# Two pads in on-chip memory that shift the buffers which TensorE reads

## The chip, the cores and the metric

The kernel runs on one core of one Trainium2 chip. The metric is the device time of one execution in microseconds; the three runs of the kernel before took 944.46, 943.92 and 945.84 us, median 944.46.

A core has TensorE (matrix products, with a separate load of the stationary operand ahead of each), VectorE, ScalarE, GpSimd and SyncE, which here issues the transfers. They share an on-chip memory of 128 partitions; a tensor takes the same range of bytes in every partition. In this text "+32" means: the tensor's first byte lies 32 bytes behind a multiple of 128.

## What is computed

Two transformer blocks in a row on 256 tokens of width 1024, in float32. The first block is a two-layer network, the second one layer with a gated linear attention. Cut to its outline:

```python
def first_block(x, ...):
    h = x
    for layer in range(2):
        if layer < 1:
            h = h + short_conv_mixer(rms_norm(h, ...), a_w_in, a_conv, a_w_out)   # 1024 -> 3072 -> 1024
        else:
            h = h + mla_attention(rms_norm(h, ...), b_w_dq, ..., k_nope, v, k_rope, cos, sin)  # 8 heads
        h = h + conv_ffn(rms_norm(h, ffn_norm[layer]), ...)                        # 1024 -> 5632, conv, 2816 -> 1024
        if layer == 0:
            shared = shared_latent_kv(h, ...)
    return rms_norm(h, final_norm)

def second_block(x, c, ctx, ...):
    # modulation from c @ ada_w; context of 256 tokens
    a_lat, a_ctx = modulate(rmsnorm(h_lat, ...), ...), modulate(rmsnorm(h_ctx, ...), ...)
    _, o_lat = gla_mixer(a_ctx, a_lat, ...)            # 4 heads, both directions, chunks of 64
    h_lat = h_lat + mod_l[2] * o_lat
    h_lat = h_lat + mod_l[5] * sqrelu_mlp(modulate(rmsnorm(h_lat, ...), ...), mlp_w1, mlp_w2)   # 1024 -> 4096 -> 1024
    return rmsnorm(h_lat, final_g)
```

## The kernel before

Activations are kept feature-major: 128 features per chunk on the partitions, 256 tokens beside each other, so a chunk is 1024 bytes per partition and chunk k of a buffer begins k x 1024 bytes behind its start.

The weights come as a stream of "units" of 128 x 1024 float32, each of eight 128 x 128 blocks, into a ring of four slots (`raw`). ScalarE rounds a unit to the product's format (`whi`, line 1007), VectorE takes the rest (`wlo`, line 1528). Activations are split the same way into a hi and a lo buffer. A block product is then three matmuls: whi with the hi activation, whi with the lo, wlo with the hi (lines 498, 499 and 502, helper `units`), each with the weight block stationary and the 256 tokens moving. A unit is therefore 24 matmuls. Every matmul loads its own stationary operand. `looped` runs the same helper in a hardware loop; the two-layer network's up projections are 44 units each, the down projections 24 units with 22 blocks per output tile, so 528 matmuls.

Variants of it:

- Lines 477 to 481, 596 to 602, 651 to 653, 713 to 715 and 904 to 906 are the same three matmuls in another order over chunks or heads.
- Where a value matrix is wanted token-major (helper `moving`, lines 530 to 532), an activation chunk is stationary and 512 weight columns move.
- In the MLP (helper `units` with `both`, lines 501 and 502) the hi and lo halves of the activations, which lie in one buffer, move in one matmul of 2 x 256 columns, and a narrow matmul with wlo follows.
- The first units of the MLP (lines 958 to 960) read `uhi`, whose chunks are 258 columns (1032 bytes) long.
- Scores, attention values, statistics and the decays of the gated attention are plain float32 matmuls.

The order on every engine is written out by hand; engines wait for each other by semaphores. Transfers of weights are issued by SyncE as slots of `raw` come free.

On-chip tensors are placed one behind another in the order of the `sb(...)` calls, each size rounded up to 32 bytes; an `ExitStack` that is closed gives its range back, so tensors of different stages overlap. `sb` is called with a number of 4-byte columns. The program has no other say in an address. The places that matter, in bytes within a partition:

| tensors | begins before | behind a multiple of 128 | after | behind a multiple of 128 |
|---|---|---|---|---|
| raw, whi, wlo, h | 1152, 17536, 33920, 50304 | +0 | the same | +0 |
| ct (tables) | 60224 | +64 | the same | +64 |
| wa2r, t1, rstd, ssum, sq | 72032 ... 81248 | +96 | the same | +96 |
| state | 88096 | +32 | the same | +32 |
| x (hi and lo) | 96288 | +32 | 96384 | +0 |
| y, o, q, k, kn, vv, c, E, ki, kz, gv, m, ... | 112672 and on | +32 | 96 further | +0 |
| cv, sil, prod, side | 161856 and on | +64 | 96 further | +32 |
| rt_tab, c32, rstd_c | 195200 and on | +0 | 96 further | +96 |
| z (hi, lo) | 210048, 218240 | +0 | 210176, 218368 | +0 |
| uhi, ulo | 186400, 194656 | +32, +96 | 96 further | +0, +64 |

Of the kernel before, what the change touches and what calls it, by code (L numbers as in the profile page):

```python
# [17 lines left out]
F32 = mybir.dt.float32  # L18
# [159 lines left out]
def program(nc, stream, xT, ctxT, vec, cst, rot, wa2, crow, out):  # L178
    ctx = ExitStack()

    def sb(name, cols, dt=F32, stack=ctx, rows=P):
        return stack.enter_context(nc.sbuf_tensor(name, [rows, cols], dt))

    with ctx:
# [19 lines left out]
        ee = sb("ee", 4 * GH)  # L204
        state = sb("state", 2 * GH * T)

        stage = ExitStack()
        x2 = sb("x2", 2 * DC * T, F32R, stage)
        xhi, xlo = x2[:, 0:DC * T], x2[:, DC * T:2 * DC * T]
        stage.close()  # L210
        stage = ExitStack()
# [3 lines left out]
        stage = ExitStack()  # L215
# [7 lines left out]
        stage = ExitStack()  # L223
# [4 lines left out]
        stage = ExitStack()  # L228
# [3 lines left out]
        stage = ExitStack()  # L232
# [26 lines left out]
        stage = ExitStack()  # L259
        sb("stacks_held", EARLY, F32, stage)  # L260
        rt_tab = sb("rt_tab", NROT, F32, stage)
        c32 = sb("c32", DC * T, F32, stage)
        rstd_c = sb("rstd_c", T, F32, stage)
        zhi = sb("zhi", DC * T, F32R, stage)
        zlo = sb("zlo", DC * T, F32R, stage)
        stage.close()
        stage = ExitStack()
# [22 lines left out]
        stage = ExitStack()  # L290
# [2092 lines left out]
```

How the kernel before makes its waits and increments, by code:

```python
    def take(self, sem, by=1):  # L140
        self.n[sem.name] = self.n.get(sem.name, 0) + by
        self.eng.wait_ge(sem, self.value(sem))
# [6 lines left out]
    def again(self, sem, back=0):  # L150
        if self.n.get(sem.name, 0) - back > 0:
            self.eng.wait_ge(sem, self.value(sem, -back))
# [207 lines left out]
        @block.sync  # L361
# [1 line left out]
            def load_group(first, done):  # L363
                for j in range(RING):
                    sp.wait_ge(slots_done, done + (j + 1))
                    sp.dma_start(raw[:, j * D:(j + 1) * D], stream[first + j]).then_inc(raw_ready[j], 16)
# [15 lines left out]
            def load_next(p):  # L382
                sp.wait_ge(slots_done, p - RING + 1)
                sp.dma_start(raw[:, p % RING * D:(p % RING + 1) * D], stream[p]).then_inc(raw_ready[p % RING], 16)
# [11 lines left out]
            def load_down(first, last):  # L396
                for p in range(first, last):
                    load_next(p)
                    kind, u = ORDER[p]
                    if kind == "w" and u in SIDE_BEHIND:
                        s = SIDE_BEHIND[u]
                        if s >= SIDE:
                            sp.wait_ge(side_done, s - SIDE + 1)
                        sp.dma_start(side[:, s % SIDE * D:(s % SIDE + 1) * D], stream[POSITIONS + s])\
                            .then_inc(side_ready[s % SIDE], 16)
# [13 lines left out]
                sp.wait_ge(ev("out_chunk"), n + 1)  # L420
                sp.dma_start(out[:, first * T:last * T], h[:, first * T:last * T]).then_inc(ev("stored"), 16)
            sp.wait_ge(ev("stored"), 16 * len(OUT_PARTS))
```

## Time and profile before

| | |
|---|---|
| median of the runs | 944.46 us |
| span of the profiled execution, first to last instruction | 944.4 us |
| its mean granted TensorE clock | 0.997 |
| TensorE matmuls | 933.6 us busy, 6952 instructions |
| TensorE weight loads | 889.8 us busy, 6952 instructions |
| VectorE | 798.0 us busy |
| ScalarE | 564.0 us busy |

The profile gives no duration of the execution beyond the span; the median is 0.1 us above it. Busy time counts overlapping instructions once. A matmul's duration in the profile reaches over the starts of the next ones, so the cost of a matmul in a stream is the distance between starts, to be had from the timeline or from the number of matmuls that a window holds.

### The profile page before, as it was taken

What the parts mean: (1) busy time and instruction counts of PE and PEld (TensorE: products, weight loads), DVE (VectorE), ACT (ScalarE), POOL (GpSimd) and SP (SyncE); (2) the same over time, 40 slices, a digit from 0 to 9 for tenths busy, and PEclk for the clock granted to TensorE, in tenths of its full rate; (3) what the DMA queues carried; (4) which work ended last, traced back from release to release, by engine and by line L of the source; (5) the groups of instructions that cost most, each with busy time, mean ns of one, the idle gap of its engine ahead of it and who ended that gap; (6) DMA issues with size and microseconds to landing.
All of it is one profiled execution on the core that took longest, in us unless ns stands there. A gap on an engine that the chain in (4) does not pass through costs nothing.

```text
span 944.4 us, 19749 instructions
## 1 busy us (share of the span) xinstructions
PE 933.6 (99%) x6952; PEld 889.8 (94%) x6952; DVE 798.0 (85%) x1317; ACT 564.0 (60%) x934; POOL 1.8 (0%) x8
## 2 busy tenths in 40 slices
PE   9999999999999999999999999999999999999997
PEld 8999999999999999999999999988899988888886
DVE  6999899999989888899999987955868889886553
ACT  6645656666455665766666556977533668674342
POOL 0000000000000000000000000000000000000000
PEclk9999999999999999999999999999999999999998
DMA  8776575557776554565557765563674348776661
GB/s 296 245 268 229 184 273 193 195 181 277 250 269 208 174 180 157 179 199 179 183 192 269 250 241 180 175 225 134 222 252 173 112 158 265 234 236 223 180 199 44
DMA packets 53877, 195.49 MB, mean 207 GB/s; under 512 B 6110, under 2 KB 6366, under 8 KB 53696
## 3 DMA queue, kind: packets, MB, share of 16 engines
q1 hardware_dynamic: 53680, 193.72, 61.5%
q10 hardware_dynamic: 144, 1.05, 0.3%
q8 instruction: 35, 0.57, 0.2%
q14 instruction: 18, 0.15, 0.0%
HBM read 193.69 MB, written 1.05 MB: 206 GB/s over the span
## 4 chain that ended last, share of the span: by engine, by line
PE 94%; DVE 4%; ACT 1%; issue 1%; DVEq 0%; ACTq 0%
PE ps L502 25%; PE ps L498 20%; PE ps L499 19%; PE ps L501 10%; PE ps L530 2%; PE ps L532 2%; PE ps L531 2%; DVE wlo L1528 1%; PE ps L609 1%; PE ps L792 1%; PE ps L808 1%; PE ps L651 1%; PE ps L652 1%; PE ps L653 1%; PE ps L674 1%
## 5 line engine op out<-in xcount | busy, mean ns | idle before, releaser
L1528 DVE TENSOR_TENSOR wlo<-raw,whi 128x1024 fp32r<-128x1024 f32 x303 | 367.0, 1220 | 72.9 <-ACT whi L1007 71.8
L1007 ACT ACTIVATE whi<-raw 128x1024 fp32r<-128x1024 f32 x303 | 317.0, 1052 | 90.8 <-PE ps L502 58.9
L502 PE MATMUL ps<-x,wlo 128*128 128x256 f32 x1248 | 349.5, 280 | 0.0
L498 PE MATMUL ps<-x,whi 128*128 128x256 f32 x1024 | 289.1, 282 | 0.0
L499 PE MATMUL ps<-x,whi 128*128 128x256 f32 x1024 | 286.9, 280 | 0.0
L502 PEld LDWEIGHTS ps<-x,wlo 128*128 128x128 f32 x1248 | 234.9, 188 | 0.0
L498 PEld LDWEIGHTS ps<-x,whi 128*128 128x128 f32 x1024 | 192.8, 188 | 0.8 <-issue 0.2
L499 PEld LDWEIGHTS ps<-x,whi 128*128 128x128 f32 x1024 | 192.8, 188 | 0.6 <-issue 0.5
L502 PE MATMUL ps<-yhi,wlo 128*128 128x256 f32 x400 | 112.1, 280 | 0.0
L498 PE MATMUL ps<-yhi,whi 128*128 128x256 f32 x400 | 112.1, 280 | 0.0
L499 PE MATMUL ps<-ylo,whi 128*128 128x256 f32 x400 | 112.1, 280 | 0.0
L1053 ACT ACTIVATE cv<-U,vt 128x256 f32<-128x256 f32 x88 | 44.9, 511 | 85.4 <-DVE U L1672 85.4
L501 PE MATMUL ps<-x,whi 128*128 128x512 f32 x224 | 78.1, 393 | 1.0 <-DVE mr L2212 0.6
L501 PE MATMUL ps<-m,whi 128*128 128x512 f32 x224 | 77.7, 392 | 0.0
L498 PEld LDWEIGHTS ps<-yhi,whi 128*128 128x128 f32 x400 | 75.3, 188 | 0.0
L499 PEld LDWEIGHTS ps<-ylo,whi 128*128 128x128 f32 x400 | 75.3, 188 | 0.0
L502 PEld LDWEIGHTS ps<-yhi,wlo 128*128 128x128 f32 x400 | 75.3, 188 | 0.0
L502 PE MATMUL ps<-m,wlo 128*128 128x256 f32 x256 | 71.6, 280 | 0.0
L501 PEld LDWEIGHTS ps<-x,whi 128*128 128x128 f32 x224 | 42.0, 188 | 11.0 <-DVE wlo L1528 1.0
L501 PEld LDWEIGHTS ps<-m,whi 128*128 128x128 f32 x224 | 42.1, 188 | 9.3
L502 PEld LDWEIGHTS ps<-m,wlo 128*128 128x128 f32 x256 | 48.0, 188 | 0.0
L1570 DVE SCALAR_TENSOR_TENSOR cv<-U,vt,cv 128x256 f32<-128x256 f32 x96 | 45.9, 479 | 0.6 <-ACT cv L1153 0.6
(333 smaller groups left out, 1536.6 us busy)
## 6 DMA issues: line engine op xcount, KB each, us to landing
raw<-stream SPq DMA_DIRECT2D x343, 512.0 KB, 4.0
side<-stream SPq DMA_DIRECT2D x16, 512.0 KB, 4.7
h<-xT SPq DMA_DIRECT2D x2, 512.0 KB, 6.1
c<-ctxT ACTq DMA_DIRECT2D x1, 1024.0 KB, 6.2
out<-h SPq DMA_DIRECT2D x4, 256.0 KB, 2.4
ct<-cst SPq DMA_DIRECT2D x1, 898.5 KB
rt_tab<-rot SPq DMA_DIRECT2D x1, 704.0 KB
state<-crow SPq DMA_DIRECT2D x1, 512.0 KB, 6.5
```

What stands on the lines that cost most here:

```text
L498: pe.matmul(dst, whi[:, w], at(hi, k), start=(k == 0), stop=False)
L499: pe.matmul(dst, whi[:, w], at(lo, k), start=False, stop=False)
L501: pe.matmul(ps[t % lag][:, :], whi[:, w], halves_of(both, k), start=(k == 0), stop=False)
L502: last = pe.matmul(dst, wlo[:, w], at(hi, k), start=False, stop=(k == K - 1))
L530: pe.matmul(dst, hi[:, tok], whi[:, w], start=first, stop=False)
L531: pe.matmul(dst, lo[:, tok], whi[:, w], start=False, stop=False)
L532: last = pe.matmul(dst, hi[:, tok], wlo[:, w], start=False, stop=final)
L609: pe.matmul(ps[7][:, 0:T], U[:, 0:P], U[:, 0:T], start=True, stop=True)
L1007: c.sig(act.activation(whi[:, s * D:(s + 1) * D], raw[:, r * D:(r + 1) * D], ACT.Copy), hi_ready)
L1053: c.sig(act.activation(at(cv, j), U[:, j * (T + 2) + 2:(j + 1) * (T + 2)], ACT.Copy, scale=vt_col(i * 12 + (base + 3 * j + 2))), tap_ready)
L1528: c.sig(dve.tensor_tensor(wlo[:, w], raw[:, r], whi[:, w], ALU.subtract), slots_done)
L1570: c.sig(dve.scalar_tensor_tensor(out=at(cv, j), in0=U[:, o + 1:o + T + 1], scalar=w1, in1=at(cv, j), op0=ALU.mult, op1=ALU.add), seq_dve)
```

## The change

Two tensors are declared that nothing reads or writes: 24 columns (96 bytes) ahead of the stage buffers, and 8 columns (32 bytes) ahead of z.

```diff
@@ -204,6 +204,7 @@
         ee = sb("ee", 4 * GH)
         state = sb("state", 2 * GH * T)
 
+        sb("line_pad", 24)
         stage = ExitStack()
         x2 = sb("x2", 2 * DC * T, F32R, stage)
         xhi, xlo = x2[:, 0:DC * T], x2[:, DC * T:2 * DC * T]
@@ -261,6 +262,7 @@
         rt_tab = sb("rt_tab", NROT, F32, stage)
         c32 = sb("c32", DC * T, F32, stage)
         rstd_c = sb("rstd_c", T, F32, stage)
+        sb("z_pad", 8, F32, stage)
         zhi = sb("zhi", DC * T, F32R, stage)
         zlo = sb("zlo", DC * T, F32R, stage)
         stage.close()
```

The instructions of every engine and their order are the same before and after, and only addresses differ; in the profile after, a line behind the first pad has a number higher by one, behind the second by two. The table above lists the addresses. Not every operand of a product ends at a multiple of 64: the tables, the gate's weights and inputs, the sums of squares and the state keep their places, the rotary table goes from +0 to +96, and the chunks of uhi begin 1032 bytes apart.

## Rows read from the trace of the kernel before

**Rows 1.** The page: busy time, TensorE's granted clock in 40 slices, the chain by engine.

```profile
PE 933.6 (99%) x6952; PEld 889.8 (94%) x6952; DVE 798.0 (85%) x1317; ACT 564.0 (60%) x934; POOL 1.8 (0%) x8
...
PEclk9999999999999999999999999999999999999998
...
PE 94%; DVE 4%; ACT 1%; issue 1%; DVEq 0%; ACTq 0%
```

**Rows 2.** Waits of TensorE: total us, times, longest.

```profile
PE ps L609 <- DVE U L1792: 2.0, 1, 2.0
PE ps L567 <- ACT sq L1500: 0.7, 1, 0.7
```

**Rows 3.** TensorE's groups by form: count, busy us, mean ns.

```profile
L502 PE MATMUL ps<-x,wlo 128*128 128x256 f32 x1248 | 349.5, 280 | 0.0
...
L530 PE MATMUL ps<-whi,zhi 128*128 128x512 f32 x48 | 19.0, 395 | 0.0
...
L530 PE MATMUL ps<-whi,x 128*128 128x512 f32 x32 | 12.8, 400 | 0.0
```

**Rows 4.** Windows, TensorE alone: length, busy (count), clock, DMA share, GB/s.

```profile
104.50:224.50 120.00, 120.00 (x1025) 1.00 0.63 213
...
370.00:381.00 11.00, 11.00 (x94) 1.00 0.49 161
391.00:511.00 120.00, 120.00 (x1013) 1.00 0.58 193
...
658.00:676.00 18.00, 18.00 (x81) 1.00 0.51 171
740.30:754.50 14.20, 14.20 (x121) 1.00 0.54 179
800.00:900.00 100.00, 100.00 (x579) 1.00 0.69 219
924.60:935.50 10.90, 10.90 (x95) 1.00 0.00 0
```

**Rows 5.** Timeline, start and duration: z moving; a pair in the MLP.

```profile
749.90 0.28 PE L502 MATMUL ps<-zhi,wlo 128*128 128x256 f32 x1
...
750.98 0.28 PE L502 MATMUL ps<-zhi,wlo 128*128 128x256 f32 x1
...
849.78 0.39 PE L501 MATMUL ps<-m,whi 128*128 128x512 f32 x1
850.01 0.28 PE L502 MATMUL ps<-m,wlo 128*128 128x256 f32 x1
```

**Rows 6.** Weight loads by tile: ns min/median/max, first and last start.

```profile
L498 PEld LDWEIGHTS ps<-zhi,whi x48: 188/192/192, 576.1 to 754.2; 128*128 128x128 f32 x48
...
L904 PEld LDWEIGHTS ps<-zhi,whi x24: 186/192/193, 730.5 to 739.8; 128*128 128x128 f32 x24
...
L498 PEld LDWEIGHTS ps<-x,whi x1024: 187/188/193, 15.1 to 716.3; 128*128 128x128 f32 x171
```

**Rows 7.** Timeline, starts of wide matmuls, x and then z stationary.

```profile
623.60 0.40 PE L530 MATMUL ps<-whi,x 128*128 128x512 f32 x1
...
624.77 0.40 PE L532 MATMUL ps<-wlo,x 128*128 128x512 f32 x1
...
670.16 0.39 PE L530 MATMUL ps<-whi,zhi 128*128 128x512 f32 x1
...
671.29 0.39 PE L532 MATMUL ps<-wlo,zhi 128*128 128x512 f32 x1
```

**Rows 8.** VectorE's groups by form: count, busy us, mean ns.

```profile
L1615 DVE SCALAR_TENSOR_TENSOR raw<-raw,cr 128x1024 f32<-128x1024 f32 x32 | 38.8, 1219 | 0.0
...
L1633 DVE SCALAR_TENSOR_TENSOR side<-side,cr 128x1024 f32<-128x1024 f32 x16 | 19.2, 1220 | 0.0
...
L2019 DVE SCALAR_TENSOR_TENSOR x<-a,mod,x 128x256 fp32r<-128x256 f32 x16 | 7.3, 480 | 0.8 <-ACT x L1285 0.8
...
L1748 DVE SCALAR_TENSOR_TENSOR c<-c,gmod,rstd_c 128x256 f32<-128x256 f32 x8 | 3.8, 480 | 0.0
```

## The prediction

> **What bounds the kernel now.** I read the page first: TensorE is busy for 933.6 of 944.4 us at a granted clock of 2.4 GHz almost throughout, and the chain of waits runs over it for 94% [rows 1]. The waits of TensorE confirm it: the longest is 2.0 us, at the very start, and the later ones are at most 0.7 us [rows 2]. So it does not matter here how early data is ready. What matters is the distance from one matmul's start to the next. The groups by form give the counts: nearly all matmuls are "narrow" (256 moving columns, a weight block stationary) in the triples of lines 498, 499 and 502, and they differ only in the activation buffer that they read (the largest group, line 502 with x, has 1248) [rows 3]. Their mean of 280 ns is no cost, since they overlap. The distance comes from the windows: a window of length L that holds nothing but such matmuls counts about (L + 0.28)/c of them, the 0.28 us being one that began before it. That gives, from [rows 4]:
>
> - 104.5 to 224.5 us, x moving, first up projection: 120.28/1025 = 117.3 ns
> - 391 to 511, x moving, second up projection: 120.28/1013 = 118.7
> - 370 to 381, o moving: 11.28/94 = 120.0
> - 740.3 to 754.5, z moving: 14.48/121 = 119.7, or 120 by its starts: 749.90 to 750.98 holds nine distances of 120 ns [rows 5]
>
> **The experiment that before already holds.** The weights whi and wlo begin at a multiple of 128 bytes. x, y, o, c, k and m begin 32 bytes behind one. z alone, of the activations, begins at a multiple of 128. So z shows today what the others will be after. It shows two things.
>
> First, as moving operand z is not faster. It runs at 120 ns, against 117.3 and 118.7 for most of the others. The weight loads say the same: those ahead of z's narrow matmuls have a median of 192 ns in each of its stages; those of x have 188 [rows 6]. That a buffer at +32 reached 120 too, in one stretch, says that 120 is one of several steady cycles. z's narrow matmuls have it in all their stages (576 to 754 us), whatever ran before.
>
> Second, as stationary operand z is faster. Where the weights move (512 columns, lines 530 to 532), x gives starts at 623.60 and 624.77 with five distances between them, 234 ns each. z gives 670.16 and 671.29, 226 ns each [rows 7]; the means by form differ the same way, 400 to 395 ns [rows 3].
>
> **The change part by part.** No instruction is added, dropped or moved on any engine, and no wait. The first pad shifts every tensor behind `state` by 96 bytes; the second is 32 bytes and brings z to a multiple of 128 again. So the whole price is in durations.
>
> *Narrow matmuls*, which go from +32 to +0. Counts are from the units, 24 matmuls each. I take 120 ns for all of them, as z has.
>
> - Until 295 us: 24 + 8 + 44 + 22 + 3 = 101 full units' worth, 2424 matmuls, 117.35 to 120: 2424 x 2.65 ns = +6.4 us
> - 295 to 388 us (the latents, queries and o): 480 matmuls, partly at 120 already, so between 0 and +1.3; I take +0.6
> - 390 to 576 us: 44 + 22 units, 1584 matmuls at 118.7: x 1.3 ns = +2.1
> - 590 to 722 us: x in 17 units, 408 matmuls, at the rate of the stage before: +0.5
> - the last four units (924.6 to 935.5, 11.18/95 = 117.7 ns): 96 x 2.3 = +0.2
>
> Together +9.8 us.
>
> *Wide matmuls with an activation stationary*: x 96 and k 24 go from 234 to about 227 (18.39/81 in 658 to 676 [rows 4]): 120 x -7 ns = -0.8 us.
>
> *The MLP*, 448 pairs of one wide (both halves moving) and one narrow matmul, lines 501 and 502. The pair takes 2 x 100.34/579 = 346.6 ns [rows 4], of which the wide has about 230 [rows 5] and so the narrow 117. At +0 I expect the narrow at 120 and the wide at 227, which gives 347 again: 0. If only the narrow one changes: 448 x 2.6 = +1.2. If only the wide one does: 448 x -3 = -1.3.
>
> *Other products*: fp32 ones (scores, values, statistics) keep their cost. The raw units' uhi has chunks of 1032 bytes, so its chunks stay off the line whatever the buffer's start; ct, t1, ssum, sq and state stay at +32 to +96 as well, since they lie ahead of the pad. I put 0 on them, and +-0.2 at most for ulo, which moves from +96 to +64.
>
> *VectorE and ScalarE*: cv, sil, prod and side go from +64 to +32 and c32 from +0 to +96. The rows show no price for a start. Three-operand products of 128x256 take 480 ns on c (+0), 480 on x (+32); products of 1024 take 1220 on side (+64) and 1219 on raw (+0) [rows 8]. ScalarE is busy for 60% only [rows 1]. So 0, and TensorE's slower pace would cover some ns anyway; without that cover, one ns on each of VectorE's 1317 instructions would be 1.3 us.
>
> Sum: 9.8 - 0.8 = +9.0 us. Nothing covers it, as TensorE is the bound. The profiled execution spans 944.4 us, 0.1 under the median of 944.46, so I add to the latter: **953.5 us**.
>
> **A rule against it.** Rows 7 show that a start at +32 and one at +0 give different distances for a stationary operand. The Trainium skill (SBUF — State Buffer, Specifications) puts the line of on-chip memory at 16 bytes and charges for each crossing to a new line. All starts here, before and after, are multiples of 32, so by that rule the pads change nothing, and the time stays 944.5. The trace disagrees for the stationary operand (234 against 226 ns); for the moving one it leaves the rule a chance, below.
>
> **The rivals.**
>
> *No difference* (0.2). The cycle is set by how a stretch was entered and not by the address. For it: the same buffer x at the same address runs at 117.3 in the first block and at 118.7 in the second, and o, also at +32, at 120.0 [rows 4]. Against it: z was entered several times, after fp32 products and after wide ones, and has 120 in all of them [rows 6]. Then only the stationary gain is left, and the MLP at 0: 943.7 us. The cadences of the first block stay at 117.3. The time that the rule above gives lies within 0.2% as well.
>
> *Faster* (0.25 in all). It is one mechanism: a moving operand that begins at a multiple of 128 bytes takes less time, as a stationary one does, and z's 120 is a coincidence of its stage. Its place is every narrow matmul, and it decides if the distance at +0 is under 117.3. The mild form: all stages settle at 117.3. Then 390 to 576 us gives -2.1, o and the latents -0.6, the x units -0.5, z's 216 x -2.6 = -0.6, the stationary ones -0.8, the MLP -1.3: -5.9 us, 938.6 us. The strong form: each narrow matmul saves the 7 ns that the stationary operand shows, on 4992 + 216 of them and the MLP's 448: about -40 us, 905 us. Against both stands that z shows the opposite. I give the mild one 0.2 and the strong one 0.05.
>
> *The MLP is hit too*, inside the forecast: 954.7; or the wide one gains: 952.2.
>
> **How the numbers follow.** Forecast 0.55, no difference 0.2, faster 0.25. About 0.2%, 1.9 us, is what a measurement can tell here. The forecast is wholly above it, "no difference" wholly within, so slower 0.55, same 0.2, faster 0.25. The forecast's own range is 949 (only the first block changes) to 955.5 (the MLP's narrow ones, the upper bound of 295 to 388 us, and noise). With "no difference" and the upper edge of the mild gain the range is 941 to 955.5; what is left out is the rest of "faster", about 0.2.
>
> **What would show it.** In the profile after, the window 104.5 to 224.5 should count about 1002 matmuls instead of 1025, and the starts there should be evenly 0.12 us apart. The weight loads of x should have a median of 192 ns. Lines 530 to 532 with x should stand 0.226 us apart, and a pair in the MLP at 0.347. The forecast is wrong if the count in that window is 1025 or more; if it is, the time is 944 or below. It is also wrong if z, now at +256 of 512 instead of +128, leaves 120.

## The result and the profile after

| | before | after |
|---|---|---|
| median of 6 runs | 945.83 us (943.92 to 947.93) | 957.92 us (954.83 to 958.49) |
| ratio | | 1.0123, 95% interval 1.0105 to 1.0141 |
| span of the profiled execution | 944.4 us | 956.4 us |

The change makes the kernel slower by 1.2%. The six runs of after lie at two levels, 954.8 to 954.9 and 957.6 to 958.5; the profiled execution took 958.23 us, so it is one of the upper level. Its time is 1.8 us longer than its span.

The page of after, against [rows 1]:

```profile
PE 945.8 (99%) x6952; PEld 899.8 (94%) x6952; DVE 799.3 (84%) x1317; ACT 563.8 (59%) x934; POOL 1.8 (0%) x8
...
PE 94%; DVE 4%; ACT 1%; issue 1%; DVEq 0%; ACTq 0%
```

The counts are the same and TensorE is busy for 12.2 us more; the other engines' busy time changed by at most 1.3 us. So the matmuls stand further apart. The windows over the same stretches of work, moved on by what the kernel has lost until there, answer to [rows 4]:

```profile
106.50:226.50 120.00, 120.00 (x1002) 1.00 0.62 209
376.50:387.50 11.00, 11.00 (x94) 1.00 0.47 164
400.00:520.00 120.00, 120.00 (x1002) 1.00 0.57 190
668.00:686.00 18.00, 18.00 (x79) 1.00 0.52 171
812.00:912.00 100.00, 100.00 (x568) 1.00 0.65 216
```

The first and the third hold 1002 narrow matmuls where before had 1025 and 1013: 120.28/1002 = 120.0 ns in both blocks, and the starts are evenly 0.12 us apart. The second, o moving, was at 120 already. The weight loads agree: x's median is now 192 ns, as z's was in [rows 6], and z's has fallen to 188:

```profile
L500 PEld LDWEIGHTS ps<-x,whi x1024: 188/192/192, 15.2 to 725.5; 128*128 128x128 f32 x171
```

```profile
L500 PEld LDWEIGHTS ps<-zhi,whi x48: 187/188/192, 584.7 to 763.2; 128*128 128x128 f32 x48
...
L906 PEld LDWEIGHTS ps<-zhi,whi x24: 186/188/192, 739.6 to 749.0; 128*128 128x128 f32 x24
```

z was to stay as it was, since it begins at a multiple of 128 before and after. It did not. Where [rows 5] had 120 ns, the 119 distances between these two starts are 118.7 ns each:

```profile
749.44 0.28 PE L500 MATMUL ps<-zhi,whi 128*128 128x256 f32 x1
...
763.56 0.28 PE L504 MATMUL ps<-zhi,wlo 128*128 128x256 f32 x1
```

x and z have changed roles as stationary operands too (line 532 of after, which is line 530 of before: 397 ns with x and 400 with z, where [rows 3] had 400 and 395); z's wide stage holds 79 matmuls in 18 us where it held 81.

The last window is the other surprise: the pair of the MLP takes 2 x 100.34/568 = 353.3 ns, where before had 346.6. Its timeline, against [rows 5]:

```profile
859.79 0.40 PE L503 MATMUL ps<-m,whi 128*128 128x512 f32 x1
860.03 0.28 PE L504 MATMUL ps<-m,wlo 128*128 128x256 f32 x1
860.15 0.40 PE L503 MATMUL ps<-m,whi 128*128 128x512 f32 x1
860.39 0.28 PE L504 MATMUL ps<-m,wlo 128*128 128x256 f32 x1
860.50 0.40 PE L503 MATMUL ps<-m,whi 128*128 128x512 f32 x1
860.73 0.28 PE L504 MATMUL ps<-m,wlo 128*128 128x256 f32 x1
860.85 0.40 PE L503 MATMUL ps<-m,whi 128*128 128x512 f32 x1
```

Three pairs take 1.06 us, and it is the wide one that grew. Over the starts of the whole down half of the MLP its mean distance to the narrow one behind it is 236.0 ns, where before had 229.2; the narrow one's is 117.3, where before had 117.5.

Where the 12 us between the two spans went, from the starts of the same instruction in the two traces (in us; stretches by the time of before):

| stretch | before | after | difference |
|---|---|---|---|
| 7.8 to 296.7, first block's narrow | 288.92 | 295.35 | +6.4 |
| 296.7 to 391, attention | 94.42 | 94.58 | +0.2 |
| 391 to 576, second block's narrow | 184.64 | 186.72 | +2.1 |
| 576 to 768, gated attention | 192.5 | 192.9 | +0.4 |
| 768 to 923, the MLP's pairs | 154.89 | 157.67 | +2.8 |
| 923 to 936, its last narrow ones | 12.53 | 12.82 | +0.3 |

### The profile page after: what moved, and what is told of

Its sections match the earlier page's. It is cut to its first block, busy times and chain, and to the rows that moved or that the text cites. A ratio compares the mean times of both kernels' runs of the same rounds, so it can differ in the third digit from the quotient of the medians.

```text
span 956.4 us, 19749 instructions
## 1 busy us (share of the span) xinstructions
PE 945.8 (99%) x6952; PEld 899.8 (94%) x6952; DVE 799.3 (84%) x1317; ACT 563.8 (59%) x934; POOL 1.8 (0%) x8
## 4 chain that ended last, share of the span: by engine, by line
PE 94%; DVE 4%; ACT 1%; issue 1%; DVEq 0%; ACTq 0%
PE ps L504 25%; PE ps L500 20%; PE ps L501 20%; PE ps L503 10%; PE ps L532 2%; PE ps L534 2%; PE ps L533 2%; DVE wlo L1530 1%; PE ps L611 1%; PE ps L794 1%; PE ps L810 1%; PE ps L653 1%; PE ps L654 1%; PE ps L655 1%; PE ps L676 1%
## 5 line engine op out<-in xcount | busy, mean ns | idle before, releaser
L504 PEld LDWEIGHTS ps<-x,wlo 128*128 128x128 f32 x1248 | 238.8, 191 | 0.0
L501 PEld LDWEIGHTS ps<-x,whi 128*128 128x128 f32 x1024 | 196.5, 192 | 0.6 <-issue 0.5
L500 PEld LDWEIGHTS ps<-x,whi 128*128 128x128 f32 x1024 | 196.5, 192 | 0.6 <-issue 0.5
L503 PEld LDWEIGHTS ps<-x,whi 128*128 128x128 f32 x224 | 42.1, 188 | 12.0 <-DVE wlo L1530 0.8
```

The lines of the kernel that those rows point to most:

```text
L500: pe.matmul(dst, whi[:, w], at(hi, k), start=(k == 0), stop=False)
L501: pe.matmul(dst, whi[:, w], at(lo, k), start=False, stop=False)
L503: pe.matmul(ps[t % lag][:, :], whi[:, w], halves_of(both, k), start=(k == 0), stop=False)
L504: last = pe.matmul(dst, wlo[:, w], at(hi, k), start=False, stop=(k == K - 1))
```

## The experiments

In all of them a tensor's "distance" is where it begins behind the place of the weights (whi; wlo has the same), modulo 256 bytes. It isn't to be mixed up with the distance of starts in time, which is given in ns and is called the pace below; a pace that a stretch of matmuls keeps is a steady cycle. Before: x, y, o, c, k, m at 160, z at 0. After: x, y, o, c, k, m at 0, z at 128.

**A map of distances.** All work is left out but the three patterns of products, on two large buffers, the activation's start moved by 32 bytes from one section to the next; each section is 96 narrow, 36 wide or 48 pair matmuls behind a short float32 product. VectorE and ScalarE do nothing while they run, and next to nothing is transferred (0 to 3 GB/s, where the long stages of the kernel have about 200).

```python
for kind, ws, xs in plan():
    w0, xb = 8 * ws, x0 + 8 * xs        # columns of 4 bytes
    pe.matmul(ps[6][:, 0:64], ones[:, :], ones[:, 0:64], start=True, stop=True)
    ...
    pe.matmul(dst, W[:, w], X[:, hi], start=(k == 0), stop=False)
    pe.matmul(dst, W[:, w], X[:, lo], start=False, stop=False)
    pe.matmul(dst, W[:, wl], X[:, hi], start=False, stop=(k == 7))
```

> Leaves out the whole computation: it only runs the three patterns of products (narrow triples, wide with the activation stationary, pairs of the MLP) with the activation buffer begun at 16 places 32 bytes apart (0 to 480 bytes behind the weights' place, modulo 512), and the narrow one also with the weights moved on by 128, 256 and 384 bytes. Theory 'distance' (what counts is where the moving operand begins against where the stationary one does, modulo 256 or 512): narrow 120 ns at distance 0 and 118.7 or less at the others; with the weights moved by 128 the 120 moves with them, to activations at +128. Theory 'place' (the activation's own place modulo 512 counts): the 120 stays at the same activation place whatever the weights do. Theory 'multiple of 128' (my prediction's): 120 at 0, 128, 256 and 384 alike. Wide: 227 ns at distance 0, 233 at 128 by both of the first theories, 227 at both by the third. Pair: 353 ns at distance 0 and 346.6 at 416 (where before had it).

The rows are the products between the sections, in order of time; the distances are 0, 32, 64, ... 224 bytes, each from one row to the next:

```profile
28.68 0.33 PE L75 MATMUL ps<-ones 128*128 128x64 f32 x2
40.41 0.33 PE L75 MATMUL ps<-ones 128*128 128x64 f32 x2
51.85 0.33 PE L75 MATMUL ps<-ones 128*128 128x64 f32 x2
63.38 0.33 PE L75 MATMUL ps<-ones 128*128 128x64 f32 x2
75.12 0.33 PE L75 MATMUL ps<-ones 128*128 128x64 f32 x2
86.86 0.33 PE L75 MATMUL ps<-ones 128*128 128x64 f32 x2
98.48 0.33 PE L75 MATMUL ps<-ones 128*128 128x64 f32 x2
109.59 0.33 PE L75 MATMUL ps<-ones 128*128 128x64 f32 x2
121.17 0.33 PE L75 MATMUL ps<-ones 128*128 128x64 f32 x2
```

The 96 matmuls take 11.73 us at distance 0, 11.44 at 32 and 11.11 at 192. The mean pace in each section, without its first matmuls, in ns (a pair counts as one):

| distance | 0 | 32 | 64 | 96 | 128 | 160 | 192 | 224 |
|---|---|---|---|---|---|---|---|---|
| narrow, first sweep | 120.0 | 116.7 | 117.8 | 120.0 | 120.0 | 118.7 | 113.3 | 118.3 |
| narrow, other order | 120.0 | 116.7 | 117.8 | 120.0 | 118.7 | 118.7 | 117.8 | 118.3 |
| wide, activation stationary | 226.7 | 233.3 | 233.3 | 234.4 | 233.3 | 233.3 | 228.9 | 233.3 |
| pair | 353.3 | 346.7 | 353.3 | 350.1 | 351.1 | 346.8 | 353.3 | 353.5 |

The values for 256 to 480 bytes repeat these in the first sweep for narrow and wide. (In the other order 288 gave 117.8 where 32 gave 116.7, and the pair gave 346.7 at 256 where it gave 353.3 at 0.) With the weights moved on by 128, 256 or 384 bytes, the six sections at distance 0 all have 120.0, and the six at 128 have 118.7 or 120.0; the activations at their first place have 120.0 with the weights at theirs and 118.7 once the weights are 128 on. So the place alone is out, and so is a multiple of 128: distance 0 has 120.0 in every section, whatever the two places, and 128, as much a multiple of 128 as 0 is, has 118.7 in half of its sections. It isn't a sharp test, since 128 has 120.0 in the other half; moving only the weights in the kernel, below, is one. The expectation "118.7 or less at the others" failed: 96 has 120.0 in both sweeps. Two values for the same two addresses (at 128, 192 and 288) are what no theory of addresses alone allows. As the other engines stand still here, a clash with their reads and writes is not what makes these differences.

**The second pad left out.**

```diff
-        sb("z_pad", 8, F32, stage)
```

> One part alone: the first pad stays, the second is left out, so z begins at +32 (224 of 512) and all else is as after. Theories 'distance' and 'place': z's narrow matmuls at 117.3 to 118.7 ns and its wide ones at 231 to 233, about as after (118.7 and 232.5), so the time is within 0.5 us of after. 'Multiple of 128': z after and before should have been alike, which the profile after already denies; under it nothing is forecast.

957.0 us, ratio 1.012 (1.0086 to 1.0154) over before, so the first pad alone carries the loss. One thing came out otherwise than expected: z, now at distance 96, has 120.0 ns as moving operand (100 distances between the starts at 749.40 and 761.41), not 117.3 to 118.7, which is what the map has for 96. Its profile fell on a run of the lower level (955.52 us, span 953.7), and the MLP, whose buffers lie exactly where after has them, is as fast as before:

```profile
809.50:909.50 100.00, 100.00 (x578) 1.00 0.70 221
```

That is 347 ns for a pair, at the address that has 353.3 in after. In the down half the wide one is at 231.8 and the narrow one at 114.8 ns. So the same instructions at the same addresses have two paces in two executions, though of kernels that differ in z's place.

**The second pad alone**, with z put where after has it:

```diff
+        sb("z_pad", 32, F32, stage)
         zhi = sb("zhi", DC * T, F32R, stage)
```

> The other part alone: before, with 128 bytes ahead of z, so that z begins at a multiple of 128 (256 of 512), as after, and all else is as before. If the second pad costs what the traces show in z's wide stages (48 x 3 matmuls at +5.5 ns, +0.8 us) less what z's narrow ones give back (216 x -1.3 ns, -0.3 us), the time is +0.5 us over before; x at 117.3 and 118.7 as before, the MLP's pair at 346.6. Theory 'multiple of 128': no difference at all.

946.17 us, ratio 1.000 (0.9981 to 1.0019): no difference that can be measured. By the starts, z's wide stages lost 0.7 us and its narrow one gained 0.2, as expected. The profile, of a run of 947.12 us, also held what was not: until 103 us x and y, at their unchanged places, ran at 118.7 ns where the trace of before has 117.3, and from there at before's pace; the stretch from 7.8 to 103 us took 1.5 us longer. And o, also unmoved, ran at 117.3 ns where before had 120.0.

**Everything moved by 128 bytes**, the weights too:

```diff
+        sb("first_pad", 32)
         raw = sb("raw", RING * D)
```

> After, with 128 more bytes ahead of the very first buffer: all buffers, the weights' too, move on by 128, distances stay. Theory 'distance': as after, narrow x at 120.0 ns in all stages, the MLP's pair at 353.3, time within 0.5 us of after. Theory 'place': x is now at 256 of 512, where z had 118.7 ns after, so narrow x at 118.7 (4992 x -1.3 ns = -6.5 us) and a changed pair.

956.28 us, ratio 1.0103 (1.0069 to 1.0137). The four runs lie at after's two levels, 954.94 and 955.01, 957.54 and 957.95, so the median says little here; level by level they are within 0.5 us of after. The trace, of a run of 957.54 us, has after's windows, and its pairs in the MLP are at 353.3 ns:

```profile
106.50:226.50 120.00, 120.00 (x1002) 1.00 0.61 210
400.00:520.00 120.00, 120.00 (x1002) 1.00 0.57 191
```

**Distances and entries.** The map again, with the float32 product ahead of a section varied in width:

```python
ENTRIES = (64, 33, 97, 128, 17, 80)
for kind, d, e in plan():
    pe.matmul(ps[6][:, 0:e], ones[:, :], ones[:, 0:e], start=True, stop=True)
```

> Leaves out the whole computation, as the first map did. Each of the 8 distances 0 to 224 bytes modulo 256 (where the activations begin behind the weights' place) is entered six times for narrow triples and four times for pairs, each time behind a float32 product of another width (64, 33, 97, 128, 17, 80 columns); between 160 and 224 bytes there are also steps of 8 bytes. Theory 'distance and entry' (a distance allows one or several steady cycles, and the entry picks one): distance 0 always at 120 for narrow, 192 at 113.3 in some entries and 117.8 in others, 128 at 120 or 118.7; the pair at distance 0 at 353.3 in some and 346.7 in others, at 32 and 160 always at 346.7. Theory 'distance alone': the same value for all entries of a distance, and the second sweep of the first map then has no explanation.

| distance | settled values over the entries, ns |
|---|---|
| narrow 0 | 120.0 six times |
| narrow 32, 64, 96 | 116.7; 117.8; 120.0, each six times |
| narrow 128 | 120.0 twice, 118.7 four times (rounded) |
| narrow 160 | 118.7 seven times (rounded), 117.3 once, 120.0 once |
| narrow 192 | 117.8 six times (rounded), 113.3 three times |
| narrow 168, 184, 200 | 120.0, three times each |
| pair 0 | 353.3 once, 346.7 three times (rounded) |
| pair 32, 160 | 346.7 four times each |
| pair 192 | 353.3 four times |

The rows around distance 192 with entry widths 64 and 33, and around the pair at 0 with the same two:

```profile
63.44 0.33 PE L78 MATMUL ps<-ones 128*128 128x64 f32 x2
69.31 0.33 PE L78 MATMUL ps<-ones 128*128 128x64 f32 x2
...
110.66 0.30 PE L78 MATMUL ps<-ones 128*128 128x33 f32 x2
116.33 0.30 PE L78 MATMUL ps<-ones 128*128 128x33 f32 x2
...
471.61 0.33 PE L78 MATMUL ps<-ones 128*128 128x64 f32 x2
477.48 0.33 PE L78 MATMUL ps<-ones 128*128 128x64 f32 x2
...
518.27 0.30 PE L78 MATMUL ps<-ones 128*128 128x33 f32 x2
524.04 0.30 PE L78 MATMUL ps<-ones 128*128 128x33 f32 x2
```

The same 48 matmuls at the same addresses take 5.87 or 5.67 us, the same 32 of the pairs 5.87 or 5.77. A distance has one steady pace or several. What picks one isn't shown: it isn't the width of the product ahead alone, since 97 columns led to 117.8 ns at 192 in one section and to 113.3 in another, and in the kernel the pair's pace differs between executions with the same addresses. 160, where before has its buffers, has all three that the trace of before showed: 117.3, 118.7 and 120.0. For narrow matmuls this is the second half of the "no difference" rival, true for 160 and false for 0; the pair has two paces at 0.

**Buffers at 192**, the MLP's inner buffer at 32, as an edit of after:

```diff
-        sb("line_pad", 24)
+        sb("line_pad", 8)
-        sb("z_pad", 8, F32, stage)
+        sb("z_pad", 40, F32, stage)
+        sb("m_pad", 24, F32, stage)
         m2 = sb("m2", 2 * MC * T, F32R, stage)
```

> Pads chosen so that x, y, o, c and z begin 192 bytes behind the weights' place modulo 256 and the MLP's inner buffer and the raw units' at 32. Theory 'distance and entry': if the stages are entered into the 113.3 ns cycle, 4992 narrow matmuls gain 4.0 to 5.4 ns each, about -22 us, x's wide ones -0.5 us, the MLP's upper pairs (224, at 353.3) cost +1.5: about -21 us, 925 us. If all are entered into 117.8: about +1.0 in the first block, -1.4 in the second, +1.5 in the MLP, so +1 us. Theory 'distance alone' with the map's first value: 925 us. If the first pad's cost had nothing to do with the distance: 945 to 957.

944.25 us, ratio 0.9986 (0.9971 to 1.0001): the second case. The windows give 120.28/1020 = 117.9 and 120.28/1021 = 117.8 ns:

```profile
104.50:224.50 120.00, 120.00 (x1020) 1.00 0.64 211
391.00:511.00 120.00, 120.00 (x1021) 1.00 0.58 194
```

The 113.3 ns pace exists, and the long stages did not fall into it. Short ones did, x from 591 to 602 us for one, where the 54 distances between these starts are 113.3 ns each:

```profile
592.00 0.28 PE L481 MATMUL ps<-x,whi 128*128 128x256 f32 x1
...
598.12 0.28 PE L502 MATMUL ps<-x,whi 128*128 128x256 f32 x1
```

No way to steer into it was found. The MLP's upper pairs are at 353.3 and its lower ones at 346.7, as the map has it for 192 and 32.

**Buffers at 32**, as an edit of after:

```diff
-        sb("line_pad", 24)
+        sb("line_pad", 32)
-        sb("z_pad", 8, F32, stage)
+        sb("z_pad", 40, F32, stage)
```

> Pads chosen so that x, y, o, c, z, the MLP's inner buffer and the raw units' all begin 32 bytes behind the weights' place modulo 256. Theory 'distance and entry': narrow at 116.7 or 117.8 in every stage, the MLP's pair at 346.7, x's wide ones at 233. Against before at 117.3 and 118.7 that is -0.6 or +0.5 ns on the first block's 2424, -2.0 or -0.9 on the second's 1584: between -6 and -0.5 us, and +1 us for z's wide ones; so 939 to 946 us.

940.61 us, ratio 0.9958 (0.9937 to 0.998): faster than both kernels, with both blocks at 120.28/1031 = 116.7 ns and the pair at 346.6:

```profile
104.50:224.50 120.00, 120.00 (x1031) 1.00 0.65 217
391.00:511.00 120.00, 120.00 (x1031) 1.00 0.60 199
800.00:900.00 100.00, 100.00 (x579) 1.00 0.69 221
```

**Only the weights moved.** Before, with the activations left at their places modulo 256:

```diff
+        sb("first_pad", 40)
         raw = sb("raw", RING * D)
...
         state = sb("state", 2 * GH * T)
+        sb("line_pad", 24)
```

> Before, with 160 bytes ahead of the weights' ring and 96 behind `state`, so that the activations keep their places modulo 256 (x at +32 of 128, z at +0) and only the weights and what lies between move, by 160: x, y, o, k and m are then at distance 0 from the weights' place, though none of them begins at a multiple of 64. Theory 'distance': narrow at 120.0 ns in all stages, as after, x's wide ones at 227, and 955 to 958.5 us. Theory that a multiple of 128 or the activation's own place causes it: as before, 117.3 and 118.7 ns, 944 to 946 us.

957.03 us, ratio 1.0134 (1.0112 to 1.0157). In it x, y, o, c, k and m begin 32 bytes behind a multiple of 128, as in before, and it is as slow as after. Its trace (of a run at the lower level, 955.88 us) has after's windows for the narrow matmuls and before's pace in the MLP, 2 x 100.34/579 = 346.6 ns for a pair:

```profile
106.50:226.50 120.00, 120.00 (x1002) 1.00 0.62 209
400.00:520.00 120.00, 120.00 (x1002) 1.00 0.57 190
809.50:909.50 100.00, 100.00 (x579) 1.00 0.69 220
```

**The inner buffer at 32.** After, with one more pad:

```diff
+        sb("m_pad", 8, F32, stage)
         m2 = sb("m2", 2 * MC * T, F32R, stage)
```

> After, with 32 bytes more ahead of the MLP's inner buffer alone, which then begins 32 bytes behind the weights' place modulo 256. Theory 'distance and entry': the pairs of the MLP's down half (224) stay at 346.7 ns however they are entered, and only those of the up half can be at 353.3; the slow ones of the runs are then 1.5 us above the fast ones instead of 3, so 954.9 and 956.4 us, and 96 narrow ones gain 0.3 us. If the two levels of the runs after have another cause than the pairs: 954.9 and 958.3 as before this edit.

Four runs: 955.96, 956.02, 956.07 and 956.53 us, all within 0.5 us of the 956.4 forecast for slow upper pairs, none at 958. In the profile the first window is in the up half and the second in the down half:

```profile
783.00:843.00 60.00, 59.85 (x339) 1.00 0.78 243
862.00:922.00 60.00, 60.00 (x348) 1.00 0.63 203
```

**The changed kernel once more**, unedited:

> The changed kernel again, beside the two others on the same chip, for its levels: 954.9 and 958.3 us in the runs so far. In the profile the MLP's pairs are at 353.3 ns if its time is near 958.3 and at 346.7 if it is near 954.9; a time near 958.3 with pairs at 346.7 would make the theory of two cycles wrong for this difference.

957.70 to 957.75 us in four runs, ratio 1.0138 (1.012 to 1.0155), and both halves slow:

```profile
783.00:843.00 60.00, 59.85 (x339) 1.00 0.78 243
862.00:922.00 60.00, 60.00 (x341) 1.00 0.61 200
```

348 against 341 is the down half's pair at 346.7 ns against 353.3 by the starts: one pad of 32 bytes ahead of one buffer, 1.5 us. No run fell on the lower level here, so a profile of this very kernel at 954.9 us was not had; the one with the second pad left out and the one with only the weights moved stand for it. The link of the two levels to the pair rests on five traces with the activations at distance 0: the three at the upper level (957.54, 957.70 and 958.23 us) have 353.3, the two at the lower (955.52 and 955.88) have 346.7.

## Why the prediction was wrong

Its direction and its largest part were right, its size was not: 957.92 against 953.5, above the range's 955.5. Two steps make up nearly all of the 4.4 us, the MLP (2.8) and the base (1.4 by the medians). By its steps:

- **Narrow matmuls, +9.8 us.** Right in size: +6.4 in the first block and +2.1 in the second, to the digit. The attention gave +0.2 where I took +0.6. That 120 held was partly luck: z's 120 could be carried over to x only because x went to z's distance from the weights, which I did not look at.
- **The MLP, 0 with a bound of +1.2.** This step failed, by 2.8 us. I composed the pair from parts measured elsewhere (120 and 227) and bounded it by leaving one part unchanged. Neither bound allows a wide matmul that grows, and it went from 229.2 to 236.0 ns, with the narrow one at 117.3, in the traces of the upper level; in those of the lower it is 231.8 and 114.8. The pair is a pattern of its own with two paces at distance 0, 353.3 and 346.7 ns, and neither holds the 120 or the 227. At the lower level the MLP costs the 0 that I put on it, and the executions there (954.83 and 954.94) lie inside the range.
- **The base.** I took the span of 944.4 for the profiled execution's own time, 0.1 from the median. But 1.8 us of after's time lie outside its span, and 1.7 to 1.8 us in every later execution of before that has its time beside its span (946.15 us and 944.4, for one). So the profiled execution of before took about 946.2, and the sum of the trace belonged to that: 946.2 + 9.0 + 2.8 is 958.0, against 958.23. The median of before also moved from 944.46 to 945.83 with three more runs.
- **z stays, x's wide ones gain 0.8.** The gain came: k's wide matmuls at 317 us take 0.25 us less and x's at 623 us 0.4 less. But z did not stay: its wide ones lost 0.7 us, what its distance 0 had been worth, and its narrow ones gained about 0.3. The prediction named a z that leaves 120 as a sign that it is wrong.
- **VectorE, ScalarE: 0.** Right: 1217 and 1219 ns for the products on raw and side, 479 on c.

The reason behind the right term was wrong. I read z's 120 ns as the mark of a multiple of 128. z had two properties, a multiple of 128 and distance 0 from the weights, which began at a multiple of 128 as well. Moving the weights alone parts them, and the distance decides. The forecast of no difference that I drew from the rule of 16-byte lines in the Trainium skill (SBUF — State Buffer, Specifications) did not hold either: with every buffer's start at a multiple of 32, 32 bytes more ahead of one buffer take 1.5 us off the MLP's down half.

The rival "no difference" was right in its fact, that a buffer at one address runs at several paces, and wrong in its conclusion: for narrow matmuls that holds at 160, where before is, while 0 had 120.0 in every section and stage. "Faster" did not come, but pads that do it exist: 32 bytes more in the first and 128 more in the second, 0.4% under before.

What stays open: why a distance has the paces that it has, and what picks one. Before has more than one level too: its executions took 943.4 to 946.8 us, with a few at 948 to 950. A step of 2 us would fit 1584 matmuls at 117.3 or at 118.7 ns; that is argued, as both traces at hand with before's places for x (about 946.2 and 947.12 us) have 118.7 in the second block, and they differ in the first 103 us. That the long stages of a kernel keep to what the map's short sections show was tested at 0, 32, 160 and 192 only.

## What to carry to other kernels

When TensorE is the bound and every matmul loads its own weights, measure the distance of starts for each buffer pair before judging a layout, and sweep the distance between the two operands over 256 bytes in a kernel that runs nothing else, with more than one entry for each, and look in the kernel itself which of the paces its stages took; here that is what lies between a 1.2% loss and a 0.4% gain. Align to what was measured, not to a round number. Before a part seen in one stage is carried to another, ask what else it has in common with its neighbours, and do not compose a pattern's pace from the paces of its parts.

## What the runs showed of the hardware

- For 256 moving and 128 stationary float32 columns, with a weight load ahead of every matmul, the pace was 113.3 ns (at 192) to about 120.7 (at 216) by the distance of the operands' first bytes modulo 256, at a granted clock of 1.00 throughout.
- With the 512 weight columns moving, 226.7 ns at distance 0 and 228.9 to 234.4 at the others: the best distance for this pattern is among the worst for narrow matmuls (120.0).
- One distance has up to three steady paces (117.3, 118.7, 120.0 ns at 160). In before x kept 117.3 for the whole first up projection and 118.7 for the whole second; at 192 the two paces lie 4.5 ns, 4%, apart.
- A pair of a 512- and a 256-column matmul at distance 0 took 346.7 or 353.3 ns in different executions with the same addresses, 3 us over 448 pairs.
- At 8 bytes beside 192 (184 and 200) the pace is 120.0, so the effect is not one of 32-byte steps alone.
